# A two-block float32 transformer kernel on one core: x, h and the branch operands start at shifted addresses

## What is computed

```python
def _swiglu(x, w1, w3, w2):
    return (jax.nn.silu(x @ w1) * (x @ w3)) @ w2
...
    for l in range(DEPTH):
        h = _swiglu(x, ffn_w1[l, 0], ffn_w3[l, 0], ffn_w2[l, 0])
        x = _layernorm(ALPHA * x + 0.5 * h, ln_g[l, 0], ln_b[l, 0])
        h = _mixer(x, l, w_in[l], ...)
        x = _layernorm(ALPHA * x + h, ln_g[l, 1], ln_b[l, 1])
        h = _swiglu(x, ffn_w1[l, 1], ffn_w3[l, 1], ffn_w2[l, 1])
        x = _layernorm(ALPHA * x + 0.5 * h, ln_g[l, 2], ln_b[l, 2])
```

## Time and profile before

| | before |
|---|---|
| median of 3 runs | 1883.05 us |
| lowest and highest | 1882.73 and 1884.14 us |
| the profiled execution | 1883.17 us |
| its span, first to last instruction | 1881.5 us |
| mean granted TensorE clock | 0.995 of full speed |
| TensorE busy with matmuls | 1849.3 us, 12859 instructions |
| TensorE busy with weight loads | 1664.8 us |
| VectorE busy | 1125.6 us |
| ScalarE busy | 890.5 us |
| GpSimd busy | 245.4 us |
| read from HBM | 327.51 MB |

### The profile page before, as it was taken

The page is one execution under the profiler, slowest core; times in us unless marked ns, Lnnn a source line. Parts: engine busy times, 40 slices in busy tenths (PEclk is TensorE's granted clock), DMA queues, the critical chain, the costliest instruction groups (busy, mean ns, idle before and its releaser), DMA issues.

```text
span 1881.5 us, 31147 instructions
## 1 busy us (share of the span) xinstructions
PE 1849.3 (98%) x12859; PEld 1664.8 (88%) x12859; DVE 1125.6 (60%) x1703; ACT 890.5 (47%) x1437; POOL 245.4 (13%) x261
## 2 busy tenths in 40 slices
PE   9999999999999999999999999999998999999999
PEld 8998699999899879987899997999775787889999
DVE  5554586676655465655675776565653645565553
ACT  5544344664455434543435653455344345454443
POOL 1000232111200020001321212000111712100000
PEclk9999999999999999999999999999998999999999
DMA  8555654445656565665745455665444223356553
GB/s 280 188 195 201 227 180 162 152 146 191 202 182 207 194 201 181 226 201 176 250 157 179 135 180 198 206 212 181 167 130 128 90 81 100 113 168 191 180 186 106
DMA packets 252397, 330.58 MB, mean 176 GB/s; under 512 B 13162, under 2 KB 213072, under 8 KB 252256
## 3 DMA queue, kind: packets, MB, share of 16 engines
q1 hardware_dynamic: 248240, 315.31, 51.5%
q0 software_dynamic: 4016, 13.27, 2.1%
HBM read 327.51 MB, written 1.05 MB: 175 GB/s over the span
## 4 chain that ended last, share of the span: by engine, by line
PE 64%; issue 23%; DVE 5%; DMA 3%; POOL 2%; ACT 2%; SPq 1%; DVEq 0%; POOLq 0%; ACTq 0%
PE bank L675 15%; PE bank L678 15%; PE bank L676 15%; PE bank L698 4%; PE bank L700 4%; PE bank L701 4%; DMA G<-in_lam_dram 1%; DVE X L1897 1%; DMA raw<-in_w_in_dram 1%; DVE wlo L1825 1%; PE bank L1231 1%; SPq L644 1%; POOL rs L2420 1%; ACT whi L1361 1%; PE bank L1209 1%
## 5 line engine op out<-in xcount | busy, mean ns | idle before, releaser
L1825 DVE TENSOR_TENSOR wlo<-raw,whi 128x1024 fp32r<-128x1024 f32 (+1 forms) x557 | 687.2, 1239 | 427.8 <-ACT whi L1361 425.6
L1361 ACT ACTIVATE whi<-raw 128x1024 fp32r<-128x1024 f32 (+1 forms) x569 | 594.2, 1050 | 429.8 <-PE bank L678 189.7
L675 PE MATMUL bank<-XTh,whi 128*128 128x256 f32 x2048 | 589.4, 288 | 2.0 <-DVE XTl L1834 2.0
L676 PE MATMUL bank<-XTl,whi 128*128 128x256 f32 x2048 | 579.9, 283 | 0.0
L678 PE MATMUL bank<-XTh,wlo 128*128 128x256 f32 x2048 | 579.9, 283 | 0.0
L675 PEld LDWEIGHTS bank<-XTh,whi 128*128 128x128 f32 x2048 | 392.2, 191 | 7.1 <-DVE XTl L1834 2.7
L676 PEld LDWEIGHTS bank<-XTl,whi 128*128 128x128 f32 x2048 | 392.2, 192 | 1.4
L678 PEld LDWEIGHTS bank<-XTh,wlo 128*128 128x128 f32 x2048 | 392.2, 191 | 0.0
L675 PE MATMUL bank<-HCh,whi 128*128 128x256 f32 (+1 forms) x936 | 274.2, 293 | 9.1 <-ACT whi L1361 6.9
L678 PE MATMUL bank<-HCh,wlo 128*128 128x256 f32 (+1 forms) x936 | 269.1, 288 | 0.0
L676 PE MATMUL bank<-HCl,whi 128*128 128x256 f32 (+1 forms) x936 | 269.0, 287 | 0.0
(11 more groups left out here) (329 smaller groups left out, 2338.5 us busy)
## 6 DMA issues: line engine op xcount, KB each, us to landing
raw<-in_ffn_w_dram SPq DMA_DIRECT2D x131, 1024.0 KB, 5.1
raw<-in_w_in_dram SPq DMA_DIRECT2D x76, 1024.0 KB, 5.0
raw<-in_w_mod_dram SPq DMA_DIRECT2D x24, 1024.0 KB, 5.0
raw<-in_w_branch_dram SPq DMA_DIRECT2D x16, 1024.0 KB, 5.0
raw<-in_w_out_dram SPq DMA_DIRECT2D x12, 1024.0 KB, 4.9
raw<-in_w_ffn_gate_dram SPq DMA_DIRECT2D x11, 1024.0 KB, 5.1
raw<-in_w_ffn_up_dram SPq DMA_DIRECT2D x11, 1024.0 KB, 5.1
raw<-in_w_ffn_down_dram SPq DMA_DIRECT2D x8, 1024.0 KB, 5.1
```

The source lines that it names most:

```text
L675: e.matmul(o, hi[:, k, w0:w0 + nc_], xh, start=first and k == 0, stop=False)
L676: e.matmul(o, hi[:, k, w0:w0 + nc_], xl, start=False, stop=False)
L1361: e.activation(hi_part(n), raw_part(n), ACTF.Copy).then_inc(WHI.did(n), 1)
L1825: e.tensor_tensor(lo_part(n), raw_part(n), hi_part(n).bitcast(F32), ALU.subtract).then_inc(WLO.did(n), 1)
```

## The change

The starts of the halves are no longer at multiples of 1024 bytes from the weights. `shifted` allots a room 512 bytes larger than the tensor and gives out views of it that start `by` bytes inside. `X_AT` lists, for each of the six stages that x is turned for, the shift of the high and of the low half; `H_AT` the same for the five feed-forwards. The room of a low half itself starts 512 bytes (modulo 1024) off, since the room of the high half ahead of it is 512 bytes longer. `c4`, `half` and `csil` (256 bytes together) go ahead of HCh, so that HCh and HCl, and with them the branch operands and all operands of the second block, start 256 bytes later. Everything that reads or writes XTh, XTl, Hh and Hl takes the view of its stage; shapes, strides, instructions and semaphores are the same.

```diff
+X_AT = ((256, 256), (128, 128), (64, 64), (192, 192), (384, 384), (64, 320))
+H_AT = ((256, 256), (128, 128), (64, 64), (256, 0), (448, 448))
...
+    def shifted(stack, name, n):
+
+        room = sb(stack, name, [128, n * T + 128], F32R)
+        return lambda by: room[:, by // 4:by // 4 + n * T].rearrange("p (k c) -> p k c", k=n)
...
         XTf = sb(ctx, "XTf", [128, 8, T])
+        c4 = sb(ctx, "c4", [128, 8, 4], F32R)
+        half = sb(ctx, "half", [128, 16])
+        csil = sb(ctx, "csil", [128, 8, 2])
         HCh = sb(ctx, "HCh", [128, 8, 512], F32R)
         HCl = sb(ctx, "HCl", [128, 8, 512], F32R)
         spare = sb(ctx, "spare", [128, 512])
         cols = sb(ctx, "cols", [128, 128])
         sh = sb(ctx, "sh", [128, 48, 2])
-        c4 = sb(ctx, "c4", [128, 8, 4], F32R)
-        half = sb(ctx, "half", [128, 16])
-        csil = sb(ctx, "csil", [128, 8, 2])
...
-        XTh = sb(xst, "XTh", [128, 8, T], F32R)
-        XTl = sb(xst, "XTl", [128, 8, T], F32R)
+        room_h, room_l = shifted(xst, "XTh", 8), shifted(xst, "XTl", 8)
+        XH, XL = [room_h(h) for h, _ in X_AT], [room_l(l) for _, l in X_AT]
...
-        def ffn_bufs(st, name):
-            return (sb(st, name + "Hh", [128, NF, T], F32R), sb(st, name + "Hl", [128, NF, T], F32R),
-                    some(st, name + "S", 2, [128, T]), some(st, name + "Hf", 2, [128, T]))
+        def ffn_bufs(st, name, *at):
+            hh, hl = shifted(st, name + "Hh", NF), shifted(st, name + "Hl", NF)
+            S, Hf = some(st, name + "S", 2, [128, T]), some(st, name + "Hf", 2, [128, T])
+            return [(hh(h), hl(l), S, Hf) for h, l in at]
...
-            ffn1 = ffn_bufs(st, "ffn1")
+            ffn1 = ffn_bufs(st, "ffn1", *H_AT[0:3])
...
-            ffn3 = ffn_bufs(st, "ffn3")
+            ffn3 = ffn_bufs(st, "ffn3", H_AT[3])
...
-            ffn4 = ffn_bufs(fs, "ffn4")
+            ffn4 = ffn_bufs(fs, "ffn4", H_AT[4])
...
-        FFN = [ffn1, ffn1, ffn1, ffn3, ffn4]
+        FFN = [*ffn1, *ffn3, *ffn4]
...
-            def xt(k):
-                return XTh[:, k, :], XTl[:, k, :]
+            def xt(s):
+                return lambda k: (XH[s][:, k, :], XL[s][:, k, :])
```

More of the change, by code:

```diff
@@ L722, in gemm_b, with xt_b @@
                         between()
-            def xt(k):
-                return XTh[:, k, :], XTl[:, k, :]
-            def xt_b(k, t):
-                return XTh[:, k, t * 128:(t + 1) * 128], XTl[:, k, t * 128:(t + 1) * 128]
+            def xt(s):
+                return lambda k: (XH[s][:, k, :], XL[s][:, k, :])
+            def xt_b(s):
+                return lambda k, t: (XH[s][:, k, t * 128:(t + 1) * 128], XL[s][:, k, t * 128:(t + 1) * 128])
             def turn_x(s, t):
@@ L848, in mixer @@
                 ready = x_ready(s)
-                gemm_b(("V", l), 8, 1, xt_b, (0, 1), [[4, 5], [6, 7]], 1024, lambda k, t: ready(k, (t,)), tail=3, between=turn_ws)
+                gemm_b(("V", l), 8, 1, xt_b(s), (0, 1), [[4, 5], [6, 7]], 1024, lambda k, t: ready(k, (t,)), tail=3, between=turn_ws)
                 for b in range(4, 8):
@@ L863, in mixer @@
                     empty(b)
-                    gemm_a(bank[b][:, 0:T], xt, ("qk", l, n), ready=ready if n == 0 else None)
+                    gemm_a(bank[b][:, 0:T], xt(s), ("qk", l, n), ready=ready if n == 0 else None)
                     emptied[b] = ((AMX, ("qk", l, n)),)
@@ L881, in mixer @@
                     empty(b)
-                    gemm_a(bank[b][:, 0:T], xt, ("u", l, n))
+                    gemm_a(bank[b][:, 0:T], xt(s), ("u", l, n))
                     emptied[b] = ((AMX, ("u", l, n)),)
@@ L885, in mixer @@
                         rotate(15)
-                gemm_b(("val", l), 8, 1, xt_b, (0, 1), [[4, 5], [6, 7]], 1024, tail=2)
+                gemm_b(("val", l), 8, 1, xt_b(s), (0, 1), [[4, 5], [6, 7]], 1024, tail=2)
                 for b in range(4, 8):
@@ L940, in mixer @@
                     empty(b)
-                    gemm_a(bank[b][:, 0:T], xt, ("gate", l, n))
+                    gemm_a(bank[b][:, 0:T], xt(s), ("gate", l, n))
                     emptied[b] = ((AMX, ("gate", l, n)),)
@@ L1342, in tensor @@
                     at[6] = turn_rows
-                ffn_up(2 * l, xt, x_ready(3 * l), at)
+                ffn_up(2 * l, xt(3 * l), x_ready(3 * l), at)
                 ffn_down(2 * l)
@@ L1347, in tensor @@
                 layernorm(3 * l + 1, (2, 8)[l])
-                ffn_up(2 * l + 1, xt, x_ready(3 * l + 2), ffn_mods(2 * l + 1))
+                ffn_up(2 * l + 1, xt(3 * l + 2), x_ready(3 * l + 2), ffn_mods(2 * l + 1))
                 ffn_down(2 * l + 1, context() if l else None)
@@ L1533, in mixer @@
                     if n:
-                        high("m", XTh, n - 1, mtmp[tm[l].slot["m", n - 1]], ("m", l, n - 1))
-                high("m", XTh, 7, mtmp[tm[l].slot["m", 7]], ("m", l, 7))
+                        high("m", XH[3 * l + 1], n - 1, mtmp[tm[l].slot["m", n - 1]], ("m", l, n - 1))
+                high("m", XH[3 * l + 1], 7, mtmp[tm[l].slot["m", 7]], ("m", l, 7))
                 w.pass_b(8, 4)
@@ L2037, in mixer @@
                     if n:
-                        low("m", XTl, XTh, n - 1, mtmp[tm[l].slot["m", n - 1]])
-                low("m", XTl, XTh, 7, mtmp[tm[l].slot["m", 7]])
+                        low("m", XL[3 * l + 1], XH[3 * l + 1], n - 1, mtmp[tm[l].slot["m", n - 1]])
+                low("m", XL[3 * l + 1], XH[3 * l + 1], 7, mtmp[tm[l].slot["m", 7]])
                 w.pass_b(8, 4)
```

8 lines of the change are left out of this document (4 added, 4 removed).

## The result

| | before | after |
|---|---|---|
| median of the runs compared | 1883.55 us (4 runs, 1882.73 to 1884.14) | 1872.34 us (4 runs, 1869.50 to 1872.87) |
| ratio | | 0.9938, 95% interval 0.992 to 0.9955 |
| profiled execution, span | 1883.17 us, 1881.5 us | 1871.84 us, 1870.1 us |

The change makes the kernel 11.2 us faster, 0.6%. I had forecast 1883.1 us and no change. The time lies just inside the range, near its lower end (1871 to 1911), on the side that got a chance of 0.17.

What follows compares the result with a forecast made beforehand. TensorE, busy 98% of the span, was taken as the bound: the matmuls' own pace plus a few holes. Terms 0 + 0 + 0 on the profiled 1883.17 us gave 1883.1 us, range 1871 to 1911 us.

Steps and rivals of the forecast that it cites:

- ScalarE and VectorE: Operations writing or reading the moved halves: value 0, bound 4 us either way over six stage starts.
- instructions: All queues: nothing added, removed or reordered, only starts differ, no wait added; cost 0.
- c4 and csil: Modulation and csil products, 192 matmuls, whose operands move ahead of HCh: value 0, bound 0.9 us either way.
- x halves, h halves and branch operands: 11,448 matmuls reading shifted operands: value 0, bounds 53 us slower and 126 us faster.
- The pace is 0.1200 for both: 256-column matmuls before: distances 0 and 512 modulo 1024 both run at 0.1200 us, slice after slice.
- the narrow rows: 32-column slices and 4-column c4 products at other distances: 0.2313 us each, 4.6 ns above 226.7, laid to the narrow operand.
- the lower bound: If shifted matmuls' excess fell to plain float32's 2.3 ns, each gains 11.0 ns, 126 us in all; taken as 0.
- Both shapes pay the same 13.3 ns on top: 256- and 512-column matmuls both take 13.3 ns beyond 106.7 and 213.3 ns; held against a collision at equal homes.
- the faster rival: The 13.3 ns are a collision at equal homes: 11.6 us gained in one up stage, 126 us in all; chance 0.17.
- one relieved stage: One up stage fully relieved, 1056 matmuls by 11 ns: 11.6 us gained, to 1871.5 us.
- The slower rival: Some distances make reads meet: at 4.6 ns per matmul 5 us in one up stage, 53 us over all; chance 0.21.
- The forecast test: Profile after: unchanged paces in every up and down stage if right; a dependence on distance would show as steps between stages.

Runs made afterwards that it cites:

- run 7: Changed kernel with high and low halves of x and h at mostly different distances and HCh back at its old place: 1873.21 us, one run.
- run 5: Changed kernel with x, last h and HCh shifted 192 bytes, the first four h 0: 1843.06 us, ratio 0.9796 to before.
- run 8: Changed kernel with up stages loading 64, 32, 32, 64 columns, x at 0, 192, 0, 192, some output rows left out: 1862.64 us, one run.
- Run 9: Changed kernel with up stages at 184, 200, 188, 196, other stages at 4 to 248, HCh back: 1888.00 us beside 1881.41 before, one run.
- run 1: Changed kernel with all shifts 0 except x in the third up stage at 192, HCh back: 1875.87 us, ratio 0.9968 to before.
- run 3: Changed kernel with a 192-byte pad moving the weights and HCh, x's room kept, some x and h shifts altered: 1869.27 us, one run.
- run 2: Changed kernel with x and h shifted 192 bytes in all stages, HCh left at 256: 1852.87 us, ratio 0.984 to before.

## Why the prediction was wrong

**The bound was read rightly.** TensorE's own pace is what an edit of addresses can move, 1 ns per matmul being 11.4 us. Some 9.0 of the 11.4 us of span are that pace; the rest is the clock's interval in the third up stage (1.5 us) and the second block (1.2 us). No wait was added, the longest went from 6.9 to 5.9 us, the splits of x and h kept their durations within 1 ns, and the counts are the same. So were the terms of 0 for *ScalarE and VectorE* and for instructions right, and that of c4 and csil can't be told from 0 in the trace.

**The step that failed** is in the change part by part, *x halves, h halves and branch operands*: "Since the slice at distance 0 shows it too, I lay it to the narrow operand, not to the offset, and take 0 for the shift." For this term of 0 the runs showed 15.4 us won and 6.4 lost. Two things were wrong with it. First, the values that the trace of before held for full-width loads, 0 and 512 modulo 1024, are one value, since the pace has a period of 256 bytes (run 7, and the first up stage, whose 256 gives 120.0). "The pace is 0.1200 for both" was no evidence of insensitivity. Second, the narrow rows do not stand for wide ones. Moving HCh by 192 in run 5 takes the 32-column slices from 231.1 to 232.0 ns only, while the full-width matmuls on the same tensors go from 119.9 to 113.5 (branches) and 114.4 (second block): the row I leaned on is nearly blind to what I asked of it. And width and offset don't act apart, as I had them: in run 8 another offset is quick with 64 columns than with 128.

**"A collision of two operand streams should shrink when one of them is cut from 128 columns to 32 or 4, and there the excess grew"** was my ground for 0 at the lower bound. At the very distance, 0, in the very form, 256 columns, run 8 has it shrink: 120.0 becomes 113.3 with a load of 64 columns, and 114.0 on average with 32. At 192 it grows: 113.3 or 117.8 becomes 119.1 with 64. So the sign of the change depends on the distance, and the 18 ns of the narrow rows, of 512 columns, tell nothing of the other form. A slip in the same sum: 5.58 / 13 is 0.4292 us, 2.6 ns over twice 213.3 and not 2.3, which makes the bound 122 us instead of 126.

**"Both shapes pay the same 13.3 ns on top"**, which I held against the faster rival, was chance: at 192 the one pays 6.7 or 11.1, the other 15.6 or 20.0; at 64 they pay 11.1 and 20.0.

**The faster rival** was right in kind and wrong in size. It gave a relief of 11 ns for each matmul, 11.6 us in one up stage. The third up stage was relieved of 6.6 ns (6.9 us), the second and fourth of 2.2 (2.3 us each). No distance tried went below 113.3. That the time is near my "one relieved stage", 1871.5 us, is luck: it is made of other terms, several stages with small gains, less the losses of the second form, plus 2.7 us that are not pace.

**The slower rival** was right for the 512-column form: the old distance was the good one and the new ones cost 5.6 to 6.6 ns, near the 4.6 I had priced. The change puts 1104 matmuls of that form (two down stages, the mixers) at worse distances, which cost the 6.4 us of the table. Run 9 shows that it could have decided: with the wrong distances the kernel has 1888.0 us beside 1881.4, one run each.

**The forecast test** was right and found it: each stage has its own distance, so a dependence shows as steps by stage. The trace after shows just that.

The Trainium skill ("TensorE: Matmul & The Clock Gate", section "Step-by-step: what each phase is for") says: "Loading the next tile's weights doesn't steal SBUF read bandwidth from the running matmul." No run here measures what the reads of SBUF get. But the running matmuls are not free of what is loaded: with x at distance 0, they go at 120.0 ns with loads of 128 columns and at 113.3 with loads of 64 (run 8), and with x at 192 at 113.3 or 120.0 by where the weights start (runs 1 and 3).

**What stays open.** Shown is the dependence: on distance, on the pattern of three, and on the width of load and output together. Not shown is the mechanism, which reads meet and where. What decides between the two paces of a distance is open as well; in the traces the turns stand at other matmuls between those of the form (turned rows, L786, modulation products), at waits and at changes of the clock, which is where they happen, not why. Whether the clock's short intervals at the lower level have to do with the quicker pace was not tried.

## What to carry to other kernels

Where TensorE is busy for 98% and each matmul has a load of its own, read the pace as distance between starts over 90 or so matmuls, stage by stage, and look at the distance between loaded and streamed operand modulo 256 bytes; one pad is a cheap trial, and each form of product needs its own (here 192 for 256 columns, 0 for 512). Before values of a parameter in a trace are taken as several, ask whether they may be one, and don't let a row of another width stand for the row in question without one run that varies both. Try the points of a sweep one by one: 192 is the best and 196 the worst of them, four bytes apart. And read more than one stretch of a stage, since one distance can have two paces.

## What the runs showed of the hardware that was not expected

- The pace of back-to-back matmuls, each with a load of 128 columns, depends on the distance between the two operands' starts: 113.3 to 122.2 ns for 256 columns, 226.7 to 234.1 for 512, at the full granted clock, with a period of 256 bytes. It is the relative place that counts (run 3).
- Some distances have two paces: 192 has 113.3 and 117.8 ns (228.9 and 233.3 in the other form), 16 has 116.7 and 118.7, 208 has 116.7 and 119.2. One holds for up to 114 us (run 5, 1008 matmuls of the second block at 113.3), and every turn that I found stands where other instructions, a wait or a change of the clock come between. In the last down stage, at 192, all five traces that have it (after, runs 2, 5, 7, 8) show 113.3, 117.8, 113.3, 117.8 in its four pieces.
- With loads and outputs of 64 columns another distance is quick: 0 has 113.3 ns and 192 has 119.1 (run 8, one run).
- The granted clock drops to the lower level for 3.4 us as some stages begin. Which ones, differs between kernels: one in the first block before (from 687.8 us), two in the change (from 214.6 and 890.5), four in run 5 (from 207.6, 473.8, 675.2 and 1142.8). Each follows a layer norm. In it TensorE is busy, but with narrow matmuls: before, it began 41 in the 11.5 us up to 687.8 and waited for 0.8 us at the longest.
